# Two-block transformer step, one core: the transposes of X and B are moved between the blocks of the projection that forms them

## The reference, cut to what matters

```python
xbc = jax.nn.silu(causal_dwconv(xbc, conv_w, conv_b))        # 4096 columns of h @ w_in
xs, Bm, Cm = jnp.split(xbc, (D_INNER, D_INNER + SSD_GROUPS * D_STATE), axis=-1)   # 2048, 1024, 1024
dt = jax.nn.softplus(dt_raw + dt_bias)
X = (xs * dt[..., None]).reshape(b, c, Q, G, K, P)
a_cs = jnp.cumsum((dt * A)..., axis=-1)
CB = jnp.einsum('bclgn,bcsgn->bcgls', Cc, Bc)
y_diag = jnp.einsum('bcgkls,bcsgkp->bclgkp', CB[:, :, :, None] * Ldec, X)
states = jnp.einsum('bclgn,bcgkl,bclgkp->bcgkpn', Bc, decay_states, X)
y = y_diag + y_off + d_skip[:, None] * xs
```

## Time and profile before

| what | value |
|---|---|
| median of 3 runs | 2072.21 us (2071.46 to 2074.02) |
| the profiled execution | 2072.07 us, of which the span from first to last instruction 2070.3 us |
| granted TensorE clock, mean | 0.982 |
| TensorE busy | 1975.6 us, 95% |
| VectorE busy | 1659.4 us, 80% |
| ScalarE busy | 1303.7 us, 63% |
| DMA | 498.76 MB, 241 GB/s on average |

### The profile page before, as it was taken

One profiled execution on the slowest core, in us unless ns is written; L12 is line 12 of the kernel. 1 busy time (PEld: TensorE's weight loads), 2 busy tenths in 40 slices (PEclk: granted clock), 3 DMA queues, 4 the chain that ended last, 5 costly groups with the idle time before them and its releaser, 6 DMA issues. The chain is left out here.

```text
span 2070.3 us, 28098 instructions
## 1 busy us (share of the span) xinstructions
PE 1975.6 (95%) x11173; PEld 1699.6 (82%) x11173; DVE 1659.4 (80%) x2110; ACT 1303.7 (63%) x1943; POOL 0.2 (0%) x4
## 2 busy tenths in 40 slices
PE   7879999988999999999999999989999999999999
PEld 4768788877878888888888888869988789979997
DVE  5876898677779989998999899978755667767884
ACT  2644543366677777787878787856565745536663
POOL 0000000000000000000000000000000000000000
PEclk8988999999999999999999999999999999999999
DMA  8625699731269989998999899955422444334553
GB/s 314 241 86 192 261 365 350 273 148 41 103 233 367 360 335 357 371 357 332 359 356 370 325 363 358 356 184 186 163 102 102 163 163 144 123 104 145 188 186 111
DMA packets 70809, 498.76 MB, mean 241 GB/s; under 512 B 8080, under 2 KB 8336, under 8 KB 11408
## 3 DMA queue, kind: packets, MB, share of 16 engines
q1 hardware_dynamic: 69952, 494.28, 64.3%
q10 hardware_dynamic: 720, 2.62, 0.4%
HBM read 495.82 MB, written 1.05 MB: 240 GB/s over the span
## 5 line engine op out<-in xcount | busy, mean ns | idle before, releaser
L345 DVE TENSOR_TENSOR wlo<-ring,whi 128x1024 fp32r<-128x1024 f32 (+1 forms) x845 | 1015.5, 1216 | 234.4 <-ACT whi L393 214.0
L393 ACT ACTIVATE whi<-ring 128x1024 fp32r<-128x1024 f32 (+1 forms) x845 | 884.8, 1054 | 470.1 <-PE ps L237 385.2
L237 PE MATMUL ps<-whi,hT 128*128 128x256 f32 (+2 forms) x944 | 316.6, 335 | 10.8 <-DVE hTl L299 4.3
L237 PE MATMUL ps<-wlo,hT 128*128 128x256 f32 (+2 forms) x944 | 311.7, 330 | 0.0
L237 PE MATMUL ps<-whi,hTl 128*128 128x256 f32 (+2 forms) x944 | 311.5, 330 | 0.0
L237 PE MATMUL ps<-whi,xg 128*128 128x512 f32 (+1 forms) x768 | 289.3, 377 | 1.3 <-DVE wlo L345 1.1
L237 PE MATMUL ps<-whi,xgl 128*128 128x512 f32 (+1 forms) x768 | 285.8, 372 | 0.0
L237 PE MATMUL ps<-wlo,xg 128*128 128x512 f32 (+1 forms) x768 | 285.5, 372 | 0.0
L237 PE MATMUL ps<-whi,hf 128*128 128x512 f32 x528 | 208.3, 394 | 4.8 <-DVE wlo L345 3.1
L237 PEld LDWEIGHTS ps<-whi,hT 128*128 128x128 f32 x944 | 182.0, 193 | 33.0 <-DVE wlo L345 7.1
L237 PE MATMUL ps<-wlo,hf 128*128 128x512 f32 x528 | 205.7, 390 | 0.0
(11 more groups left out here) (299 smaller groups left out, 2597.4 us busy)
## 6 DMA issues: line engine op xcount, KB each, us to landing
ring<-in_wstream SPq DMA_DIRECT2D x462, 1024.0 KB, 4.9
ring<-in_wstream SPq DMA_DIRECT2D x4, 832.0 KB, 5.4
modrow<-in_gates ACTq DMA_DIRECT2D x3, 512.0 KB, 6.8
ring<-in_wstream SPq DMA_DIRECT2D x6, 256.0 KB, 2.6
cst<-in_cst SPq DMA_DIRECT2D x1, 1028.0 KB, 7.7
x<-in_x SPq DMA_DIRECT2D x1, 1024.0 KB, 13.1
work<-in_bias ACTq DMA_DIRECT2D x2, 512.0 KB, 5.4
ring<-in_wstream SPq DMA_DIRECT2D x2, 512.0 KB, 3.8
```

Source lines behind the costliest of these rows:

```text
L237: i = self.e.matmul(out, lhsT, rhs, start=start, stop=stop, skip_group_check=True)
L345: i = self.e.tensor_tensor(K.wlo[:, q % NS, 0:cols], src, hi.bitcast(F32), ALU.subtract)
L393: i = self.e.activation(K.whi[:, q % NS, 0:cols], K.ring[:, m % RING, at:at + cols], ACT.Copy)
```

## The change: what it does

The table `SSD_TURNS` gives each of the ten banks of transposes a block. X of columns 512n to 512n + 511 and positions 128i to 128i + 127 is turned in front of block 7 + 4n + i, B in front of blocks 25 and 29. They go to bank 6 or 7, wait for the SiLU of their four blocks, and ScalarE copies each of them out at the end of its work for that block. The section behind unit 0 of q goes; VectorE copies none.

```diff
+SSD_TURNS = {7 + 4 * n + i: (n, i) for n in range(4) for i in range(2)} | {25: (4, 0), 29: (5, 0)}
+def row_bank(n, i):
+    return 6 + (i if n < 4 else n - 4)
+def ssd_turned(K, n, i):
+    return K.X[:, i, 512 * n:512 * n + 512] if n < 4 else K.Brow[:, 512 * (n - 4):512 * (n - 4) + 512]
 def pe_ssd(K, pe):
...
+        if j in SSD_TURNS:
+            n, i = SSD_TURNS[j]
+            b = row_bank(n, i)
+            pe.take(b)
+            pe.wait_ge(K.act, ("xbc", "silu", 4 * n + 3))
+            for q in range(4):
+                pe.tr(K.ps[b][:, 128 * q:128 * q + 128], xbc[:, 4 * n + q, 128 * i:128 * i + 128], done=("row", n, i) if q == 3 else None)
+            pe.given(b, (K.act, ("row", n, i)))
     pe_cols(K, pe, "xbc", 32, "conv", ready(K, pe, "n1"), at_block=at_block)
     pe_project(K, pe, "qkv0", 0, 1, QKV0)
-    pe.wait_ge(K.act, ("xbc", "silu", 23))
-    for i in range(2):
-        for q0 in range(0, 16, 4):
-            b = next_bank(K, ("X", i, q0))
-            pe.take(b)
-            for q in range(4):
-                pe.tr(K.ps[b][:, 128 * q:128 * q + 128], xbc[:, q0 + q, 128 * i:128 * i + 128], done=("X", i, q0) if q == 3 else None)
-            pe.given(b, (K.dve if q0 % 8 else K.act, ("X", i, q0)))
-    for q0 in (0, 4):
...
-        pe.given(b, (K.act, ("B", q0)))
     pe_project(K, pe, "qkv0", 1, 3, QKV0)
     pe.wait_ge(K.dve, "XS")
-    pe.wait_ge(K.act, ("B", 4))
+    pe.wait_ge(K.act, ("row", 5, 0))
 def act_ssd(K, a):
...
+        if j in SSD_TURNS:
+            n, i = SSD_TURNS[j]
+            a.wait_ge(K.pe, ("row", n, i))
+            a.act(ssd_turned(K, n, i), K.ps[row_bank(n, i)][:, :], ACT.Copy, key=("row", n, i), own=False)
...
     act_project(K, a, "qkv0", 0, 1, QKV0, K.rows0)
-    for i in range(2):
-        for q0 in (0, 8):
-            a.wait_ge(K.pe, ("X", i, q0))
-            a.act(X[:, i, 128 * q0:128 * q0 + 512], K.ps[K.bank.get(("X", i, q0), 4)][:, :], ACT.Copy, key=("X", i, q0), own=False)
-    for q0 in (0, 4):
-        a.wait_ge(K.pe, ("B", q0))
-        a.act(Brow[:, 128 * q0:128 * q0 + 512], K.ps[K.bank.get(("B", q0), 4)][:, :], ACT.Copy, key=("B", q0), own=False)
 def dve_ssd(K, v):
...
-    for i in range(2):
-        for q0 in (4, 12):
-            v.wait_ge(K.pe, ("X", i, q0))
-            v.copy(X[:, i, 128 * q0:128 * q0 + 512], K.ps[K.bank.get(("X", i, q0), 4)][:, :], key=("X", i, q0), own=False)
-    v.wait_ge(K.act, ("X", 1, 8))
+    v.wait_ge(K.act, ("row", 3, 1))
     v.tt(heads(XD), heads(X[:, 0, :]), wide(dt[:, 0, :]), ALU.mult)
```

## The result

The changed kernel takes 2068.15 us (median of 14 runs, 2064.66 to 2071.82), the kernel before beside it 2072.31 us (14 runs). The ratio is 0.9977, with an interval of 0.997 to 0.9985: 3.1 to 6.2 us faster. The forecast was 5.5 us, a time of 2066.7 us in a range of 2065.0 to 2070.5.

The account below looks back on a forecast made before the run. TensorE was taken to set the pace in the projection. Removing the section (-10.17 us) and adding ten groups (+4.6 us) was summed as -5.5 us, so 2072.2 became 2066.7 us, range 2065.0 to 2070.5.

Parts of the forecast that it names:

- What is removed: Transpose section behind unit 0 of q: all ten banks leave, taking 10.17 us off TensorE's path, unit 1 following at once.
- What is added: Between projection blocks: ten groups of four transposes, paid in full on TensorE at 0.46 us each, 4.6 us (4.4 to 6.5).
- The neighbour of equal shape: In the later projection sproj: four transposes in a stream of 512-column matmuls, cost 0.45 us, basis for the group's price.
- the pair of small tiles: Between blocks 13 and 14: two 32-column transposes cost 0.43 us, giving 0.65 us for four as upper end.
- The cover: In the projection: ScalarE's ten copies of 0.59 us fit within the block's matmul time and cost nothing.
- What is late next: Before the state products: XS on VectorE, at most 0.1 us later, within its 1.0 us margin.
- The price of 0.65 us a group: Rival, between projection blocks: groups cost as much as beside small tiles, 2068.5 us, no measurable difference; chance 0.15.
- The slow clock moving behind the state products: Rival: slow clock falls there instead, taking back 1.7 us, 2068.4 us; chance 0.12 together with XS being late.
- Transposes in the stream slowing the clock: Rival, in the projection: each group brings a slow clock, 1.7 us ten times, 2084 us; chance 0.04.
- The rule cited from the Trainium skill: On TensorE's clock gate: a transpose does not count as work as a matmul does, speaking against the change.
- Copies that starve the stream: Rival, in the projection: ScalarE's copies make splits late, waits of 5.5 us cancel the gain, 2072 us; chance 0.05.

Follow-up runs that it names:

- e2: Changed kernel with only the eight banks of X between blocks, the two of B left behind unit 0 of q; ratio 0.9995 to the kernel before.
- e6: Kernel before, with small matmuls whose result nobody reads put into the 2.27 us halt of its transpose section; ratio 0.9995 to the kernel before.
- e1: Kernel before, its section of 40 transposes kept behind unit 0 of q but over four banks instead of two; ratio 0.9992 to the kernel before.
- e7b: Changed kernel with ScalarE copying each of the ten banks three times, each copy waiting for the last; one run, 134.54 us between the marks.
- e4: Changed kernel with VectorE instead of ScalarE copying all ten banks, at the same blocks; ratio 0.9979 to the kernel before.
- e3: Changed kernel with each group of four transposes made twice into the same bank; ratio 0.9999 to the kernel before.
- e5: Changed kernel with ScalarE copying the state products before unit 4's second split and unit 2's copies; two runs, ratios 0.9966 and 0.9969 to the kernel before.
- b1: Kernel before, unchanged, another profiled execution; its transpose section takes 10.14 us, 140.37 us between the marks.
- a1: Changed kernel, unaltered, run again on another chip; ratio 0.9970 to the kernel before.

## Why the prediction was right, point by point

**What is removed: right.** 10.17 us was the section, 10.17, 10.14 and 9.98 in three executions, and all of it went: unit 1 follows unit 0 after 0.12 us. What it was made of is clearer now, as an estimate: 4.4 us of transposes at full pace; 2.27 us of halt for the bank of unit 0 (e2 has it in full with two banks left); 0.9 us of slow clock (e6); and the rest, some 2.6 us, waits for copies with only two banks (e1 removes 3.0 us by two more banks, partly of the halt, and with it the slow clock).

**What is added: right, 0.3 us too high.** A group costs 0.43 to 0.44 us by its own step, 4.3 us for the ten in the distance between the marks, where I took 4.6. The neighbour of equal shape in the earlier trace rows had it at 0.45; the pair of small tiles, my upper end, did not apply. The working gives 0.45 us for that neighbour and then takes 0.46; and -10.17 + 4.6 is -5.57, which was written as -5.5. Neither slip moves the forecast by more than 0.1 us. The sum as measured is -10.17 + 4.30 = -5.87 us.

**The cover: right, and larger than I worked out.** Neither ScalarE's copies (e7b) nor the same copies on VectorE (e4) cost TensorE anything.

**What is late next: right.** XS ends 1.04 us ahead of the state products before and after.

**The rivals.** The price of 0.65 us a group: not so. The slow clock moving behind the state products: not so, it is 1.00 there. But e2 shows that the price of such a move is real, and why: over dense matmuls the slow clock cost more than the 0.9 us that e6 found where TensorE had waits to fill. Transposes in the stream slowing the clock: not so, with 40 or with 80 of them (e3), nor with 40 one behind the other where no halt of 2.27 us is ahead (e1, e6, one trace each). The rule cited from the Trainium skill, TensorE: Matmul & The Clock Gate, section PE-mode transpose, would have made the clock fall in e1's section; the trace there does not agree. Copies that starve the stream: not so (e7b).

**The size of the median.** The part is 5.86 us shorter in both traces; the first comparison says 4.2 us (3.1 to 6.2), the second 5.5 us by the medians (ratio 4.1 to 8.5). Both intervals hold 5.9. So the mechanism and its size are borne out by the distance between the marks; that a median of 4.2 also lies near the forecast of 5.5 says less. What keeps the medians from saying more is outside the part: the first mark comes between 1386.6 and 1397.1 us in the thirteen traces, over instructions that are the same in all of them, and what is behind it took 540.3 to 541.7. Three traces of before have it at 1386.6 to 1388.2, the two of the changed kernel at 1390.1 and 1393.9, the two of e5, which is the same up to there, at 1387.1 and 1388.6.

The clock goes with a part of this. The 25 us ahead of the first mark, in the kernel before and in the changed one:

```profile
1363.00:1388.00 25.00, 18.49 (x102) 14.51 (x103) 17.04 (x33) 12.64 (x27) 0.00 (x0) 1.00 0.44 159
```

```profile
1368.00:1393.00 25.00, 19.71 (x93) 14.72 (x92) 15.53 (x32) 12.12 (x25) 0.00 (x0) 0.86 0.36 127
```

Added up from the clock of each trace, TensorE had spent 51.2 us at the lower level by the first mark in the two traces that reach it first (b1 and the first of e5), 58.0 in the first trace of before, 64.9 in the first of the changed kernel and 68.3 in e3, which reaches it last. But a1 has 58.0 too and is 1.9 us later than before, so the clock is not all of it, and whether it is the cause of the delays or comes with them stays open. The distance behind the second mark goes the same way: it is 541.3 us or more in eight of the nine traces with the fall after 93.2 us, and 540.9 or less in the four without. That a part of the gain is given back ahead of the change is not excluded by so few traces.

## What to carry to other kernels

Where one engine sets the pace without a break, small work moved between its blocks is paid in full, so the gain is the old section less its work at full pace: here 10.17 less 4.3. Look for what a section of short operations waits for behind the queues of other engines, and move or remove that wait; moving eight tenths of the work (e2) and leaving the wait gives little, and a halt can be followed by a slow clock that outlasts it. Measure an effect of a few tenths of a per cent between two marks in the traces, since spans of one program differ by more.

## What the runs showed of the hardware that was not expected

After a halt of 2.27 us the granted clock went to its lower level (0.50 to 0.53) for some 3.4 us, in all four traces that have this halt (three of before, e2); halts of 1.39 us (e1) and 0.54 us (e6) in its place were not followed by it, in one trace each. Forty transposes with such a shorter halt among them ran at 1.00. But a halt of 2.03 to 2.08 us at one later place was followed by the lower level in nine of thirteen traces and not in four, though the work there is the same: a halt of about 2 us may or may not bring it. By e6 the slow stretch cost 0.9 us where TensorE had waits to fill. In e2, over dense matmuls, the small section with it cost 1.6 us more than the waits and transposes I had worked out.

The distance between the marks repeats to 0.01 us between executions of the changed kernel, and to 0.18 us in the kernel before, while whole spans of one program differ by 4.5 us.
